# Fourteen modulation sums as transposes and a VectorE reduction in a two-layer transformer kernel

## The reference

```python
c_act = jax.nn.silu(c)
mod = c_act @ w_ada[l] + b_ada[l]                 # 2048 -> 6 * 2048
sh1, sc1, gt1, sh2, sc2, gt2 = jnp.split(mod, N_MOD, axis=-1)
h = modulate(rmsnorm(x, g_norm_mix[l]), sh1, sc1)
...                                               # mixer (layer 1) or attention (layer 2)
x = x + gt1[:, None, :] * y
h = modulate(rmsnorm(x, g_norm_ffn[l]), sh2, sc2)
f = (jax.nn.silu(h @ w_ffn_gate[l]) * (h @ w_ffn_up[l])) @ w_ffn_down[l]   # d_ff = 5632
x = x + gt2[:, None, :] * f
```

## Time and profile before

| | |
|---|---|
| median of 3 runs | 2635.07 us (2633.29 to 2635.34) |
| profiled execution | 2635.05 us, of which 2633.4 us are its span |
| TensorE busy | 2513.3 us, 95% of the span |
| VectorE busy | 1805.9 us, 69% |
| ScalarE busy | 1080.1 us, 41% |
| granted TensorE clock over the span | 0.982 of full speed |

### The profile page before, as it was taken

The page is one execution under the profiler, slowest core; times in us unless marked ns, Lnnn a source line. Parts: engine busy times, 40 slices in busy tenths (PEclk is TensorE's granted clock), DMA queues, the critical chain, the costliest instruction groups (busy, mean ns, idle before and its releaser), DMA issues.

```text
span 2633.4 us, 33569 instructions
## 1 busy us (share of the span) xinstructions
PE 2513.3 (95%) x13086; PEld 2121.3 (81%) x13086; DVE 1805.9 (69%) x1774; ACT 1080.1 (41%) x1244; POOL 222.2 (8%) x397
## 2 busy tenths in 40 slices
PE   4869999999999999999999998898999999999999
PEld 3659547888888888889999997787888888888887
DVE  6866766887888888678675446865678655555565
ACT  2025105444334344464336555444543344444443
POOL 4411220111111111001110000000001000000000
PEclk8889999999999999999999999999999999999999
DMA  9988895888888888648875554244578655555554
GB/s 367 366 318 295 310 384 175 313 327 319 314 308 318 307 313 293 197 159 292 310 270 162 162 170 132 81 144 151 201 259 307 218 190 189 189 189 189 187 191 144
DMA packets 290569, 638.97 MB, mean 243 GB/s; under 512 B 21754, under 2 KB 34556, under 8 KB 290076
## 3 DMA queue, kind: packets, MB, share of 16 engines
q1 hardware_dynamic: 233808, 432.22, 48.4%
q0 software_dynamic: 56096, 205.02, 21.0%
q10 hardware_dynamic: 556, 0.18, 0.0%
HBM read 635.28 MB, written 2.10 MB: 242 GB/s over the span
## 4 chain that ended last, share of the span: by engine, by line
PE 83%; DVE 8%; DMA 4%; issue 2%; ACT 2%; POOL 0%; DVEq 0%; ACTq 0%; POOLq 0%
PE PS L1627 82%; DMA R<-in_w_ada 4%; DVE R L973 2%; DVE WLO L954 1%; ACT WHI L511 1%; DVE R L1521 1%; PE PS L1848 1%; PE PS L1769 0%; DVE R L1349 0%; ACT R L584 0%; DVE R L1047 0%; DVE R L1590 0%; DVE YF L1592 0%; DVE R L1374 0%; DVE H L1120 0%
## 5 line engine op out<-in xcount | busy, mean ns | idle before, releaser
L954 DVE TENSOR_TENSOR WLO<-RAW,WHI 128x1024 fp32r<-128x1024 f32 x760 | 929.2, 1225 | 683.3 <-ACT WHI L511 681.0
L511 ACT ACTIVATE WHI<-RAW 128x1024 fp32r<-128x1024 f32 x760 | 804.3, 1060 | 1150.1 <-PE PS L1627 1146.5
L1627 PE MATMUL PS<-WHI,H 128*128 128x512 f32 x3296 | 1027.8, 393 | 32.3 <-issue 18.9
L1627 PEld LDWEIGHTS PS<-WHI,H 128*128 128x128 f32 x3296 | 618.4, 189 | 164.8 <-issue 28.5
L1627 PE MATMUL PS<-WLO,H 128*128 128x512 f32 x1648 | 645.0, 391 | 0.0
L973 DVE SCALAR_TENSOR_TENSOR R<-R,CA 128x1024 f32<-128x1024 f32 x360 | 461.3, 1281 | 70.4 <-DMA R<-in_w_ada 63.2
L1627 PE MATMUL PS<-H,WHI 128*128 128x256 f32 x2656 | 490.9, 287 | 12.8 <-DVE WLO L954 11.7
L1627 PEld LDWEIGHTS PS<-H,WHI 128*128 128x128 f32 x2656 | 417.8, 193 | 19.1 <-DVE WLO L954 16.4
L1627 PE MATMUL PS<-WHI,HID 128*128 128x512 f32 x1280 | 395.8, 390 | 0.0
L1627 PE MATMUL PS<-H,WLO 128*128 128x256 f32 x1328 | 377.6, 284 | 0.0
L1627 PEld LDWEIGHTS PS<-WLO,H 128*128 128x128 f32 x1648 | 311.5, 189 | 65.9
(11 more groups left out here) (215 smaller groups left out, 1266.7 us busy)
## 6 DMA issues: line engine op xcount, KB each, us to landing
R<-in_w_ada POOLq DMA_DIRECT2D x384, 512.0 KB, 6.6
RAW<-in_w_in SPq DMA_DIRECT2D x88, 1024.0 KB, 5.9
RAW<-in_w_ffn_in SPq DMA_DIRECT2D x88, 1024.0 KB, 5.0
RAW<-in_w_ffn_gate SPq DMA_DIRECT2D x44, 1024.0 KB, 6.3
RAW<-in_w_ffn_up SPq DMA_DIRECT2D x44, 1024.0 KB, 5.2
RAW<-in_w_ffn_down SPq DMA_DIRECT2D x44, 1024.0 KB, 8.2
RAW<-in_w_ffn_out SPq DMA_DIRECT2D x44, 1024.0 KB, 5.1
RAW<-in_w_out SPq DMA_DIRECT2D x32, 1024.0 KB, 5.1
```

What stands on the lines that cost most here:

```text
L511: nc.scalar.activation(WHI[j][:, :, :], RAW[slot][:, 2 * half:2 * half + 2, :], ACT.Copy)\
L954: nc.vector.tensor_tensor(WLO[j][:, :, :], RAW[slot][:, 2 * half:2 * half + 2, :], WHI[j][:, :, :].bitcast(F32), ALU.subtract).then_inc(lo ...
L1627: return nc.tensor.matmul(o, a, b, start=start, stop=stop, skip_group_check=True)
```

## The change

From group 10 on, TensorE no longer multiplies the blocks of `ACC` with ones. `ada_turn` transposes the eight blocks into the whole of pair D (both halves, 1024 columns), and VectorE then adds up each block's 128 columns with one `tensor_reduce` into the SBUF columns `SUM8`, waits for that result on its own chain semaphore (`step`), and adds the bias to `SUM8`. Groups 0 to 9 stay as they were. Since pair D's second half is now overwritten as well, TensorE gets waits: `gate_row(1, 0)` for the last modulation bias (`ada_bias`), the feed-forward part for ScalarE's last copy of the gate row (`rows_read`, after sub 19 of its turn), and the last input-projection body for VectorE's reading of the latents' sums (`lat_ms`, after sub 12). The VectorE loop counts one more chain step in each turn.

```diff
+        SUM8 = SM[:, 16:24]
...
                 at = c.ada_group.value(0, times=8)
-                nc.vector.tensor_tensor(MOD[:, bass.ds(at, 8)], SMALL[:, 0:8], PRM[:, bass.ds(at, 8)], ALU.add)\
-                    .then_inc(ada_bias, 1)
+                if c.ada_group.at < 10:
+                    nc.vector.tensor_tensor(MOD[:, bass.ds(at, 8)], SMALL[:, 0:8], PRM[:, bass.ds(at, 8)], ALU.add)\
+                        .then_inc(ada_bias, 1)
+                else:
+                    step(nc.vector.tensor_reduce(SUM8, flat("D").rearrange("p (a b) -> p a b", a=8), AX_X, ALU.add))
+                    nc.vector.tensor_tensor(MOD[:, bass.ds(at, 8)], SUM8, PRM[:, bass.ds(at, 8)], ALU.add)\
+                        .then_inc(ada_bias, 1)
...
-                    c.enter(i - 3, unit=12, sub=24, hid=1, ada=KT * beside, ada_group=1 * beside)
+                    c.enter(i - 3, unit=12, sub=24, hid=1, ada=KT * beside, ada_group=1 * beside, chain=1 * beside)
...
                     if s == ada_after:
-                        ada_sum()
+                        ada_turn()
...
+            def ada_turn():
+                pe.wait_ge(ada_op, c.ada_group.value(1, times=KT))
+                pe.wait_ge(ada_bias, c.ada_group.value())
+                for j in range(8):
+                    ins = nc.tensor.transpose(flat("D")[:, j * P:(j + 1) * P], ACC[:, j * P:(j + 1) * P], ident)
+                ins.then_inc(ada_red, 1)
+                c.ada_group.at += 1
...
                 pe.wait_ge(diag_done, 4 * k + n + 1)
+                if k == 1 and n == 0:
+                    pe.wait_ge(ada_bias, c.ada_group.value())
...
-                down(ada_after=0 if beside else None, then=lambda n: {1: lambda: gate_row(k, 3)} if n == 0 else {})
+                rows_read = lambda: pe.wait_ge(gt_row, 4 * k + 4)
+                down(ada_after=0 if beside else None,
+                     then=lambda n: {0: {1: lambda: gate_row(k, 3)}, 1: {1: rows_read}}.get(n, {}))
...
-            group("B", ada_after=5)
+            group("B", ada_after=5, then={4: lambda: pe.wait_ge(lat_ms, 1)})
```

## The result

The changed kernel takes 2619.48 us (median of 5 runs, 2619.18 to 2622.31) against 2635.07 us: a ratio of 0.9946, 95% interval 0.9935 to 0.9957. That is 15.6 us less, where 12.0 us were forecast; it lies on the lower bound of the forecast range (2619.5 us). Run again later beside 15 runs of the kernel before, it took 2623.58 us (2618.23 to 2624.21) against 2634.86: 0.9952, interval 0.9939 to 0.9966, 11.3 us less. The profiled execution took 2620.68 us, its span 2619.0 us.

A forecast was written before the change was run, and what follows sets the result against it. TensorE was taken to bound the kernel. Eleven feed-forward and two input-projection sums at 0.91 us (11.8 us) plus 0.2 us for the third make 12.0 us: 2623.1 us, range 2620.5 to 2626.5 us, with moved clock 2619.5 to 2628 us.

The forecast's parts named there:

- TensorE's saving: At each sum, eight transposes take 0.79 us where products with ones took 1.70: 0.91 us saved, bounds 0.7 and 1.0.
- VectorE's cost: Per sum, a reduction of 1024 columns from PSUM at 1.2 us, 1.25 us with the wait behind it; covered by idleness.
- completion wait: On VectorE, between reduction and addition: some 0.05 us more per sum.
- remaining slack: VectorE's idleness before the next `lo()` at feed-forward sums: 1.2 us left of 3.33 us after the change.
- second cover: Behind VectorE's idleness at feed-forward sums: `lo()` ends 2.9 us before TensorE's sub needs it.
- The rival of a slow reduction: At the sums, reductions at the reciprocal's 6.55 us make `lo()` late: 15 us slower, 2650 us; chance 1%.
- The third sum: In the input projection, TensorE already waits for VectorE there: gain only 0.2 us, between -0.5 and +0.5.
- Nothing tells the sign: Around the attention stage, half-clock stretches may come or go: two more give 2626.5 us, two fewer 2619.7 us.
- the clock moves elsewhere: Rival: earlier arrival shifts lower-clock stretches around the attention stage, net two or more; chance 17%, 11% up and 6% down.
- The rule that spoke against it: At the new transposes, the skill page says full clock does not engage for them; by the profile, no cost.
- The other edits: New TensorE waits at gate row, its last copy and latents are met on arrival; VectorE's loop counters fit the slack: nothing.

The follow-up runs named there:

- identity products: The changed kernel with ordinary float32 products of each accumulator block with the identity in place of the transposes; 2631.97 us.
- doubled transposes: The changed kernel with each of the fourteen sets of eight transposes issued twice, the same result written again; 2632.9 us.
- the kernel with five reductions: The changed kernel with the reduction of each sum done five times, each waiting for the one before; 2682.76 us.
- the third alone: The kernel before with transposes and reduction at the third input-projection sum only, products with ones at the other thirteen; 2633.13 us, 0.9992.
- the filler: The kernel before plus eight transposes of the identity, result unread, behind the products with ones of the third input-projection sum; 2631.15 us, 0.9988.
- the waits alone: The kernel before with the three new TensorE waits (gate row, its last copy, latents) and nothing else of the change; 2634.0 us, 1.0000.
- the last five sums: The kernel before with transposes and reduction only in the three input-projection sums and the two of the second feed-forward part; 2630.49 us, 0.9982.
- the first nine only: The kernel before with transposes and reduction only in the nine sums of the first feed-forward part; 2625.96 us, 0.9968.

## Why the prediction was right

**TensorE's saving.** 0.91 us per sum from 1.70 and 0.79 was exact; the turns give 0.95 us. Eleven turns make 10.4 us, the first two sums of the projection 1.8 to 1.9 us. The identity products show that the reason is the halved number of pairs, and the doubled transposes that TensorE's time counts in full.

**VectorE's cost.** 1.2 us forecast, 1.216 us measured, covered at thirteen sums. The 0.05 us for the completion wait, for which the prediction named no row, is 0.03 us (the reduction ends at 1057.06, the addition starts at 1057.09). The remaining slack of 1.2 us was 1.11. But the second cover was mis-sized: I took the subtraction as what is late next, and named the additions of finished column blocks as queued behind it without asking who waits for them. It is the addition behind the subtraction, and 2.9 us of second cover were 1.7 us. At 1.25 us of cost that did not matter. The rival of a slow reduction was priced by that cover at 15 us above the kernel before (its 11 x 0.4 us is 4.4 and not 4.6) and would have been worse: the kernel with five reductions, 6.25 us, takes 48 us more than the kernel before.

**The third sum.** "I give this sum 0.2 us, between -0.5 and +0.5" failed. The wait took TensorE's gain as said, and the late subtraction came as said, but I measured it against a profile in which the fall of the clock had already made TensorE late. There the third of VectorE's subtractions behind the sum is held by ScalarE until 8.32 us after the sum's first record (1356.99 to 1365.31). With products with ones at full clock it starts after 6.85 us (1349.03 to 1355.88), in the changed kernel after 8.02 us. At equal clock the place costs 1.0 us: from the first big product to the start of the sub after next are 6.78 us in the changed kernel, where two subs take 5.8. The sum at equal clock is then 10.4 + 1.8 - 1.0 = 11.2 us by the trace, where the products give 12.0 us and the slope 13.0 us.

**The clock.** "Nothing tells the sign" was the other failed step. Transposes, or products with 128 columns, at the third sum raise the mean clock by 0.0009 over all kernels, and by 0.0013 and 0.0012 in the two that isolate it (the third alone, the filler). In the profiles this is worth 2.6 us, in the attention stage. The forecast had this as a rival, "the clock moves elsewhere", with 6% for the way it went. With it the forecast of 12.0 us becomes 11 to 12 at equal clock plus 0 to 3, and 11.3 and 15.6 us were the two medians. The forecast was right in size partly by luck: these two errors, 1.2 us too much at the third sum and nothing for the clock, have opposite signs.

**The rule that spoke against it.** The Trainium skill, page "TensorE: Matmul & The Clock Gate", section "Part 4: PE-mode transpose", has it that a transpose does not count as TensorE activity in the way a product does. These float32 runs do not bear it out: with eight transposes of the identity, alone, the mean clock was 0.98355 and not 0.98233. The nine sets of transposes in the first feed-forward part lowered it nowhere (clock 1.00 from 500 to 1090 us).

**The other edits** cost nothing, as forecast: 1.0000 for the waits alone.

**What stays open.** In the profiles with one-column products at the third sum only one of four showed the fall right behind it; the kernel before with the waits alone had full clock there. One fall of 3.4 us in one of four executions is too little for 0.0009. The greater part lies in the fall between the second and the third set of transposes of the attention stage, some 345 us behind the third sum, and in work that a later fall slows or spares. How eight instructions decide on it that long before is not shown. There is one profile for each kernel, and the one with the last five sums is an exception. A mere shift in time does not explain it: the filler moves the next big product by 0.01 us, and the first nine only, which shifts the stage by nearly 9 us, keeps the fall.

## What to carry to other kernels

When TensorE is the bound, count load-and-product pairs, not columns: a float32 product costs two pairs, a float32 transpose one, so a reduction over partitions may be cheaper as transposes plus a VectorE sum, where VectorE has idleness to spare. To find how much it has, follow every instruction queued behind the new one to the engine that waits for it, not only the next one of the kind that is usually late. And don't read a cost off one profile at a place where the clock has just fallen: compare over several runs, with the granted clock beside each, and find the place of the difference in the traces.

## What had not been expected of the hardware

Adding eight transposes that nobody reads (0.83 us of TensorE in place of a wait of 0.68 us) made the kernel 3.6 us faster. In its profile 2.6 us are won in the attention stage, where a fall of the clock to half is missing. A wait of 1.49 us behind transposes did not bring the clock down in the changed kernel's profile. With five reductions a wait of 2.58 us in the feed-forward part was followed by half clock for 3.4 us, behind nine of the eleven sums.
